# The low part of each weight panel on GpSimd instead of DVE

## What is computed

```python
proj = rmsnorm(x, g) @ w_in          # and split into q, k, v, gates ...
x = x + mixer(proj) @ w_out
u = rmsnorm(x, g) @ w_up
x = x + (silu(conv(gate)) * val) @ w_down
```

## Time and profile before

| | before |
|---|---|
| median of 3 runs | 4706.24 us |
| span of the profiled execution | 4705.5 us |
| PE (matmul) busy | 4033.5 us, 86% |
| DVE busy | 2084.3 us, 44% |
| ACT busy | 1342.8 us, 29% |
| GpSimd (POOL) busy | 0.2 us |
| HBM | 278.44 MB, 59 GB/s |

### The profile page before, as it was taken

How to read it: one execution, slowest core, us unless ns; L and a number is a source line. 1 busy time by engine, 2 the same in 40 slices (tenths; PEclk the granted TensorE clock), 3 DMA queues, 4 the chain that set the end, 5 groups by cost and what they waited for, 6 DMA issues and landing times. The chain is left out here.

```text
span 4705.5 us, 54624 instructions
## 1 busy us (share of the span) xinstructions
PE 4033.5 (86%) x21065; PEld 3196.7 (68%) x21065; DVE 2084.3 (44%) x3286; ACT 1342.8 (29%) x1844; POOL 0.2 (0%) x4
## 2 busy tenths in 40 slices
PE   5899998988999798699978799782599957897998
PEld 4667886767788684588866688681477734676886
DVE  2374544134445424533243433426666644524333
ACT  2353433232343323232232332213211112223222
POOL 0000000000000000000000000000000000000000
PEclk9999998975899897799987899885699966998999
DMA  2201222210122220022210122210000000021221
GB/s 98 75 0 63 96 91 81 90 54 0 63 98 93 79 82 35 36 89 92 96 67 27 63 89 98 87 48 22 5 0 0 0 9 27 0 89 63 98 96 65
DMA packets 43350, 278.44 MB, mean 59 GB/s; under 512 B 5920, under 2 KB 6816, under 8 KB 10598
## 3 DMA queue, kind: packets, MB, share of 16 engines
q1 hardware_dynamic: 36576, 266.35, 16.0%
q10 hardware_dynamic: 6662, 10.53, 0.7%
HBM read 274.76 MB, written 2.11 MB: 59 GB/s over the span
## 5 line engine op out<-in xcount | busy, mean ns | idle before, releaser
L190 PE MATMUL PS<-XH,WH 128*128 128x512 f32 (+1 forms) x2848 | 1104.3, 388 | 75.0 <-DVEq L95 34.3
L191 PE MATMUL PS<-XL,WH 128*128 128x512 f32 (+1 forms) x2848 | 1106.4, 388 | 0.0
L192 PE MATMUL PS<-XH,WL 128*128 128x512 f32 (+1 forms) x2848 | 1100.2, 386 | 0.0
L146 DVE TENSOR_TENSOR WL<-W,WH 128x2048 fp32r<-128x2048 f32 x254 | 582.0, 2292 | 1007.2 <-ACT WH L136 1002.8
L136 ACT ACTIVATE WH<-W 128x2048 fp32r<-128x2048 f32 x254 | 485.4, 1912 | 1102.3 <-PE PS L260 686.5
L190 PEld LDWEIGHTS PS<-XH,WH 128*128 128x128 f32 x2848 | 540.7, 190 | 209.0 <-issue 61.2
L192 PEld LDWEIGHTS PS<-XH,WL 128*128 128x128 f32 x2848 | 541.8, 190 | 112.0
L191 PEld LDWEIGHTS PS<-XL,WH 128*128 128x128 f32 x2848 | 540.9, 190 | 111.7
L258 PE MATMUL PS<-HH,WH 128*128 128x512 f32 (+1 forms) x1024 | 402.0, 393 | 10.5 <-DVEq L95 9.3
L259 PE MATMUL PS<-HL,WH 128*128 128x512 f32 (+1 forms) x1024 | 400.3, 391 | 0.0
L260 PE MATMUL PS<-HH,WL 128*128 128x512 f32 (+1 forms) x1024 | 399.8, 390 | 0.0
(11 more groups left out here) (437 smaller groups left out, 5045.8 us busy)
## 6 DMA issues: line engine op xcount, KB each, us to landing
W<-in_weights SPq DMA_DIRECT2D x254, 1024.0 KB, 4.8
X<-in_x ACTq DMA_DIRECT2D x1, 2048.0 KB
out<-X ACTq DMA_DIRECT2D x1, 2048.0 KB, 7.1
consts<-in_consts ACTq DMA_DIRECT2D x1, 1025.0 KB
bias<-bias_spread ACTq DMA_DIRECT2D x4, 256.0 KB
w_gd<-in_w_gd ACTq DMA_DIRECT2D x1, 640.0 KB
rope<-in_c_rope ACTq DMA_DIRECT2D x1, 528.0 KB
ws<-in_ws ACTq DMA_DIRECT2D x1, 512.0 KB
```

The costliest lines, as they stand in the source:

```text
L146: P.e.tensor_tensor(K.WL[:, s, :], K.W[:, s, :], K.WH[:, s, :].bitcast(F32), ALU.subtract).then_inc(P.sem("weights_split"), P.adds("weight ...
L190: P.e.matmul(out, wh[:, k, c], xh[:, k, r], start=(k == 0), stop=False)
L191: P.e.matmul(out, wh[:, k, c], xl[:, k, r], start=False, stop=False)
L192: last = P.e.matmul(out, wl[:, k, c], xh[:, k, r], start=False, stop=(k == KT - 1))
```

## The change

split_dve does nothing any more. A new function runs the same subtraction with the same waits and counts in a loop over all panels on GpSimd, from the start of the program to its end, outside of the stages; it takes no part in stage_done. ACT's part, the loads and TensorE's waits are as before. The waits for hi_ready leave DVE's code with the subtractions; in the narrow stages its loop stays with an empty body.

```diff
 def split_dve(K, P):
 
-    if P.split_left <= 0:
-        return
-    s = P.split_par
-    P.e.wait_ge(P.sem("hi_ready"), P.due("hi_ready"))
-    P.e.tensor_tensor(K.WL[:, s, :], K.W[:, s, :], K.WH[:, s, :].bitcast(F32), ALU.subtract).then_inc(P.sem("weights_split"), P.adds("weights_split"))
-    P.split_par ^= 1
+    pass
+
+
+def split_pool(K, P, n_panels):
+
+    def body(i):
+        for s in range(2):
+            P.e.wait_ge(P.sem("hi_ready"), P.due("hi_ready"))
+            P.e.tensor_tensor(K.WL[:, s, :], K.W[:, s, :], K.WH[:, s, :].bitcast(F32), ALU.subtract).then_inc(P.sem("weights_split"), P.adds("weights_split"))
+
+    P.loop(n_panels // 2, body, hi_ready=2, weights_split=2)
...
@@ -221,8 +229,6 @@
     if split is split_act:
         counts.update(hi_ready=2, weights_loaded0=16, weights_loaded1=16)
-    else:
-        counts.update(hi_ready=2, weights_split=2)
...
@@ -296,7 +302,7 @@
     else:
-        P.loop(whole // 2, body, hi_ready=2, weights_split=2)
+        P.loop(whole // 2, body)
...
@@ -2561,6 +2567,10 @@
+        @block.gpsimd
+        def _(e):
+            split_pool(K, engine(e, "pool"), n_panels)
```

More of the change, by code:

```diff
@@ L140, in split_dve @@
 def split_dve(K, P):
-    if P.split_left <= 0:
-        return
-    s = P.split_par
-    P.e.wait_ge(P.sem("hi_ready"), P.due("hi_ready"))
-    P.e.tensor_tensor(K.WL[:, s, :], K.W[:, s, :], K.WH[:, s, :].bitcast(F32), ALU.subtract).then_inc(P.sem("weights_split"), P.adds("weights_split"))
-    P.split_par ^= 1
+    pass
[5 more added lines that the diff above has]
+    P.loop(n_panels // 2, body, hi_ready=2, weights_split=2)
+    for s in range(n_panels % 2):
+        P.e.wait_ge(P.sem("hi_ready"), P.due("hi_ready"))
+        P.e.tensor_tensor(K.WL[:, s, :], K.W[:, s, :], K.WH[:, s, :].bitcast(F32), ALU.subtract).then_inc(P.sem("weights_split"), P.adds("weights_split"))
 def stream_sync(K, P, n_panels):
```

## The result

| | before | after |
|---|---|---|
| median of the runs made side by side (4 each) | 4705.44 us | 4736.62 us |
| lowest to highest | 4698.37 to 4707.51 us | 4735.46 to 4739.09 us |
| span of the profiled execution | 4705.5 us | 4733.7 us |

The ratio is 1.0068, with a 95% interval from 1.0054 to 1.0082: the kernel became 31 us slower. The forecast was 4736.0 us. In the kernel after, lines up to 139 keep their numbers; the two-operand additions of the norm move from L520 to L526, TensorE's mean from L501 to L507, Merge from L2207 to L2213, BiasTable's two transfers from L1108 and L1112 to L1114 and L1118.

A forecast was written before the change was run, and what follows sets the result against it. TensorE, busy 86%, with DVE's subtractions mattering only where their end releases something. Stage ends -6.5, clock -6 and norms +42.3 gave +29.8; with 0.7 added to the 4705.5 us span, 4736.0 us, range 4670 to 4763 (forecast's own 4703 to 4763).

The forecast's parts named there:

- The price of GpSimd: One panel's subtraction on GpSimd takes 4.6 us, twice DVE's row, its two operands read one after the other.
- Steady panels at nothing: In steady panels the slower subtraction is hidden: no gain, and a loss only if GpSimd needs over 6.4 us.
- The norms: Nine norms after narrow stages: two additions wait for GpSimd's subtraction, +4.7 us each, +42.3 us together.
- DVE keeps the way until its train ends: Rival: shared way into SBUF, but GpSimd waits until DVE's queued additions end; 4690.5 us, chance 0.18.
- The first rival, no contention: GpSimd reads beside DVE without waits, so only gains remain: -30.4 us, 4676 us; chance 0.24.
- Stage ends: Where the subtraction was DVE's last operation before a stage end, it leaves the path; ends sum to -6.5 us.
- the clean ends: Five places without further condition (second Store stage, QkNormRope, CentreV, two GatedNarrow stages): 5 x -2.3 = -11.5 us.
- The first norm: In the prologue, additions wait behind two GpSimd subtractions and end at 32.5: +2.9 us instead of -2.7.
- Merge: At Merge's start, its first addition (L2207) waits for GpSimd until 4253.6, now 4251.42: +2.2 us.
- BiasTable: At its start, the product L1096 would come at 1785.7 and waits for GpSimd to 1786.8: -1.2 us.
- hidden, unless P plus landing passed 22: SP's loads start 2.3 us later, at no cost unless GpSimd's subtraction time P plus load landing passes 22 us.
- The clock: TensorE's clock may not fall at four stage ends with shorter idleness: 0 to -12 us, taken as -6.

The follow-up runs named there:

- the run with the held load: Kernel after, with the 1 MB weight panel load ahead of BiasTable held until BiasTable's small transfers have landed: 4735.67 us, ratio 1.0053.
- 239 panels on GpSimd: Kernel after, with subtractions in the norms, prologue and ends before ForgettingAttention, BiasTable, CentredShift and Merge back on DVE: 4689.05 us, ratio 0.9951.
- doubling: Kernel after, with GpSimd making each subtraction twice, one after the other, into the same place: 4985.88 us, ratio 1.0595.
- the fill: Kernel after, with GpSimd filling the low part with a constant (memset, no SBUF read) in place of the subtraction: 4689.76 us, ratio 0.9962.
- GpSimd's scaling with one operand: Kernel after, with GpSimd scaling the panel by a constant in place of the subtraction, low part left out: 4725.27 us, ratio 1.0040.

## Why the prediction was right

The total, 4736.0 forecast and 4736.62 measured, is nearer than its terms.

- **The price of GpSimd.** 4.6 us forecast, 4.61 measured. The ground for it, two operands read one after the other, isn't shown: one operand takes longer (5.38 us). The Trainium skill's 4497 ns (GPSIMD Engine Reference, section 3.1, for an addition) is met exactly by the subtraction ahead of BiasTable in the run with the held load; the mean over all 254 in the kernel after is 4610.
- **Steady panels at nothing.** Shown: 104-115 in the table at 0.00, and the same time with 6 or with 239 panels on GpSimd. The slack of 6.4 us was read well enough to place the cost of doubling within 0.5 us a panel.
- **The norms.** 42.3 us forecast, 38.7 measured in the additions and 41.0 in the nine stretches. The mechanism is as told: GpSimd gets in between two additions, two of them wait for it, and everything behind moves. The wait was oversized by 0.4 us a norm: I let GpSimd start at the end of the fourth addition and take 4.6, but at this place its instruction lasts 4.51, and it starts while the fourth addition still runs. Undone alone, the norms give 40.5 us back by the spans.
- **The rival "DVE keeps the way until its train ends"** had 0.18. One row settles it: GpSimd starts at 413.61 in the middle of six additions that stand ready. It wasn't passed over here, nor in any other of the nine norms, where the additions took 8.00 us each time.
- **The first rival, no contention** (4676 us), fell with the 8.00 us of the additions. Its size was off as well: the fill, beside which the norms lose nothing, came out 19 us below the kernel before in its job (4689.76 against 4708.58), where I had put 30.
- **Stage ends.** The pattern of -2.3 us held, and at the clean ends the clock gave something on top: -3.5, -3.8 and -5.2 us in the stretches 205-207, 208-216 and 216-218 of most executions, and -5.2 at CentreV in the kernel after (-3.4 to -3.6 in six other kernels). QkNormRope lies in a stretch that moves by 5.2 us between two executions of the kernel before. The first norm was forecast at +2.9: its additions begin 2.7 us earlier, as told, and end 2.4 us later (0-2 in the table has +3.2, and moves by 1.8 between executions). Merge was forecast at +2.2 and came at +1.95. ForgettingAttention came at nothing (-0.1 forecast). CentredShift (+2.2) lies in a stretch that moves by 4.3 us between two executions of the kernel before, but its head can be read: from the start of the last split of the stage ahead to the first shift product it took 5.85 us before and takes 7.63, +1.8. Hgrn's -1.0 can't be confirmed (-0.9 in a stretch that moves by 1.4).
- **BiasTable: a missed step.** "BiasTable: the product L1096 would come at 1785.7 and waits to 1786.8: -1.2" was right for DVE. But the step on SP, "hidden, unless P plus landing passed 22", looked only at who needs the panel and not at whom the later load meets: there it met a small transfer on the path and cost 3.2 us.
- **The clock.** -6 us in one lump was a guess between bounds. Four stretches, those three and CentreV's, give 17.6 us where four subtractions give 9.2, so up to 8.4 us there is the clock's. "The clock at 1.00 behind it" failed between the two Store stages, where after 2.03 us idle it still fell to 0.50, for some 3 us. At CentreV it shows in the granted clock, 0.76 and 0.56 before and 1.00 after (by stretch, before and then after):

```profile
2495.00:2500.00 5.00, 1.07 (x2) 0.55 (x3) 2.29 (x1) 1.50 (x1) 0.00 (x0) 0.76 0.03 3
2500.00:2505.00 5.00, 5.00 (x8) 2.12 (x7) 0.00 (x0) 0.00 (x0) 0.00 (x0) 0.56 0.54 206
...
2527.00:2532.00 5.00, 2.67 (x6) 1.25 (x7) 0.00 (x0) 2.24 (x2) 2.68 (x1) 1.00 0.01 2
2532.00:2537.00 5.00, 4.46 (x11) 1.72 (x9) 0.43 (x1) 0.00 (x0) 1.81 (x1) 1.00 0.34 110
```

- **The sum.** Between the two spans, the stretch with BiasTable and DiffAttention came out 4.8 us above its term (3.2 of it the load); below theirs came the five clean ends with the clock (-21.2 against -17.5), CentredShift's stretch (+0.4 against +2.2) and the norms (1.3). And DiffAttention takes up to 10 us more or less in each execution, for which the forecast had no term. That the total came within 1 us is luck.

## What to carry to other kernels

Before moving work to an idle engine, find the places where its end releases something. Here they were eleven stage ends and nine norms among 254 panels, and six panels won as much as any other kernel here. Then look for what the new user of a shared resource meets, at its new place and length: GpSimd's subtraction holds up DVE's operations on two SBUF tensors until it has nearly ended, and that is free in a panel and 4.3 us on a dependent chain; place such an instruction behind the chain, or cut it. And when two profiles differ, run one kernel twice before a stretch is explained.

## What the runs showed of the hardware that I had not expected

- A very small operation can wait as long as a large one. At the start of Hgrn in the kernel after, a scaling of 128x8 elements from SBUF to SBUF took 4.44 us, and 0.106 in the kernel before; a 128x4 reciprocal beside a GpSimd subtraction took 0.18. A small size alone doesn't protect an operation:

```profile
1011.85 4.54 POOL L150 TENSOR_TENSOR WL<-W,WH 128x2048 fp32r<-128x2048 f32 x1 [6.48 <-ACT WH L136]
1011.98 4.44 DVE L927 TENSOR_SCALAR lbt<-lb 128x8 f32<-128x8 f32 x1
```

- That scaling waits for GpSimd's writes too. Beside the fill of 1.80 us, to which the additions are indifferent, it took 1.68 us:

```profile
997.03 1.80 POOL L150 MEMSET WL<- 128x2048 f32 x1 [9.29 <-ACT WH L136]
997.18 1.68 DVE L922 TENSOR_SCALAR lbt<-lb 128x8 f32<-128x8 f32 x1
```

- A tenth of a microsecond can decide which operation waits. In the run with only the stage ends on GpSimd, the same scaling comes 0.06 us behind GpSimd's start and takes 0.11 us; the next one takes the wait. Beside GpSimd's scaling with one operand it was the same (0.108 us, then 5.39), though it came 0.13 us behind, as in the kernel after. Why it gets through there stays open:

```profile
1000.02 0.11 DVE L992 TENSOR_SCALAR lbt<-lb 128x8 f32<-128x8 f32 x1
1000.16 4.58 DVE L942 TENSOR_SCALAR h_k<-f,lbt 128x512 f32<-128x512 f32 x1
```

- On GpSimd a scaling with one operand is slower than a subtraction with two, 5377 ns against 4610. On DVE it is the other way round.
